# A fused two-layer hybrid attention model: latent queries and keys made by feature instead of by token, their scores split into 64-row and 32-row tiles

## What is computed

```python
q = (_rmsnorm(c_q, q_norm) @ w_uq).reshape(bsz, seq, MLA_HEADS, MLA_NOPE + MLA_ROPE)   # 192 -> 8 x (64 + 32)
kv = (_rmsnorm(c_kv, kv_norm) @ w_ukv).reshape(bsz, seq, MLA_HEADS, MLA_NOPE + MLA_V)  # 128 -> 8 x (64 + 64)
q = jnp.concatenate([q[..., :MLA_NOPE], _rope(q[..., MLA_NOPE:], positions)], -1)
k_r = jnp.broadcast_to(_rope(k_rope[:, :, None, :], positions), (bsz, seq, MLA_HEADS, MLA_ROPE))
k = jnp.concatenate([kv[..., :MLA_NOPE], k_r], -1)
o_mla = _dense_causal_attention(q, k, kv[..., MLA_NOPE:], (MLA_NOPE + MLA_ROPE) ** -0.5, None)
```

## Time and profile before

| | before |
|---|---|
| median of 3 runs, us | 854.97 (854.80 to 855.01) |
| the profiled execution, us | 854.98 |
| its span in the trace, us | 853.24 |
| TensorE matmul busy | 838.6 us, 98% |
| TensorE weight loads busy | 782.6 us, 92% |
| VectorE busy | 608.9 us, 71% |
| ScalarE busy | 467.3 us, 55% |
| mean granted TensorE clock | 0.997 |

### The profile page before, as it was taken

One profiled execution on the slowest core, in us unless ns is written; L12 is line 12 of the kernel. 1 busy time (PEld: TensorE's weight loads), 2 busy tenths in 40 slices (PEclk: granted clock), 3 DMA queues, 4 the chain that ended last, 5 costly groups with the idle time before them and its releaser, 6 DMA issues.

```text
span 853.2 us, 15785 instructions
## 1 busy us (share of the span) xinstructions
PE 838.6 (98%) x6364; PEld 782.6 (92%) x6364; DVE 608.9 (71%) x1099; ACT 467.3 (55%) x714; POOL 93.4 (11%) x112
## 2 busy tenths in 40 slices
PE   7999999999999999999999999999999999999996
PEld 6899999999899999988889999999998999999885
DVE  4775777887786877765667659688878777777554
ACT  5556767664355655553437377676634465555430
POOL 1002900004500000000000155000071000000000
PEclk9999999999999999999999999999999999999998
DMA  9757443344677777465845664334356787664631
GB/s 306 201 169 241 149 141 107 108 141 158 189 198 199 197 198 197 161 222 180 265 126 152 195 204 149 122 126 135 130 182 184 192 217 195 193 193 146 239 122 49
DMA packets 176407, 148.86 MB, mean 174 GB/s; under 512 B 18156, under 2 KB 149840, under 8 KB 176336
## 3 DMA queue, kind: packets, MB, share of 16 engines
q1 hardware_dynamic: 171712, 143.08, 55.0%
q10 hardware_dynamic: 4624, 4.78, 1.9%
HBM read 146.53 MB, written 1.05 MB: 173 GB/s over the span
## 4 chain that ended last, share of the span: by engine, by line
PE 95%; DVE 3%; ACT 0%; issue 0%; DVEq 0%; POOL 0%; ACTq 0%; POOLq 0%
PE ps L644 29%; PE ps L646 28%; PE ps L645 28%; PE ps L929 3%; PE ps L960 2%; PE ps L941 2%; DVE w_lo L1453 1%; PE ps L702 1%; PE ps L908 0%; PE ps L877 0%; PE ps L909 0%; PE ps L895 0%; PE ps L1026 0%; DVE x_tok L1677 0%; ACT w_hi L1123 0%
## 5 line engine op out<-in xcount | busy, mean ns | idle before, releaser
L1453 DVE TENSOR_TENSOR w_lo<-raw,w_hi 128x2048 fp32r<-128x2048 f32 (+3 forms) x142 | 304.7, 2148 | 111.2 <-ACT w_hi L1123 111.1
L644 PE MATMUL ps<-xt_hi,w_hi 128*128 128x256 f32 x1232 | 346.1, 281 | 0.7 <-ACT fq_t L1148 0.7
L645 PE MATMUL ps<-xt_lo,w_hi 128*128 128x256 f32 x1232 | 341.4, 277 | 0.0
L646 PE MATMUL ps<-xt_hi,w_lo 128*128 128x256 f32 x1232 | 341.3, 277 | 0.0
L1123 ACT ACTIVATE w_hi<-raw 128x2048 fp32r<-128x2048 f32 (+3 forms) x142 | 252.5, 1784 | 75.6 <-PE ps L646 67.2
L644 PEld LDWEIGHTS ps<-xt_hi,w_hi 128*128 128x128 f32 x1232 | 231.7, 188 | 4.2 <-issue 3.2
L645 PEld LDWEIGHTS ps<-xt_lo,w_hi 128*128 128x128 f32 x1232 | 231.7, 188 | 0.1
L646 PEld LDWEIGHTS ps<-xt_hi,w_lo 128*128 128x128 f32 x1232 | 231.6, 188 | 0.0
L644 PE MATMUL ps<-w_hi,ht_hi 128*128 128x512 f32 x176 | 68.6, 390 | 0.0
L645 PE MATMUL ps<-w_lo,ht_hi 128*128 128x512 f32 x176 | 68.5, 389 | 0.0
L646 PE MATMUL ps<-w_hi,ht_lo 128*128 128x512 f32 x176 | 68.5, 389 | 0.0
(11 more groups left out here) (234 smaller groups left out, 1280.8 us busy)
## 6 DMA issues: line engine op xcount, KB each, us to landing
raw<-ffn_w_up SPq DMA_DIRECT2D x88, 512.0 KB, 5.1
raw<-w_in SPq DMA_DIRECT2D x84, 512.0 KB, 4.6
raw<-ffn_w_down SPq DMA_DIRECT2D x32, 512.0 KB, 4.2
raw<-w_branch SPq DMA_DIRECT2D x24, 512.0 KB, 4.7
raw<-w_out SPq DMA_DIRECT2D x16, 512.0 KB, 4.3
raw<-ffn_w_down SPq DMA_DIRECT2D x24, 256.0 KB, 3.0
ln_g<-ln_g ACTq DMA_DIRECT2D x4, 512.0 KB, 3.6
ln_b<-ln_b ACTq DMA_DIRECT2D x4, 512.0 KB, 5.4
```

The lines of the kernel that those rows point to most:

```text
L644: pe.matmul(dst, a_hi, b_hi, start=first, stop=False)
L645: pe.matmul(dst, a_hi, b_lo, start=False, stop=False)
L646: return pe.matmul(dst, a_lo, b_hi, start=False, stop=last)
L1453: ins = dve.tensor_tensor(panel_lo(l, p)[0:n, cols], panel_raw(l, p)[0:n, cols], panel_hi(l, p)[0:n, cols].bitcast(F32), ALU.subtract)
```

## The change

The 64 plain columns of each latent query and key are made by feature, like those of the other branches: `qn_t`, `kn_t` with two heads in one array of 128 rows, four arrays. Only the 32 rotated query columns are made by token (`q_rope`). The rotated key columns are copied four times side by side (`kr4`). In slot 6, four transposes of 128 columns turn `q_rope` into `qr_t` (four heads in each of two arrays, ordered so that a pair's two heads lie 64 rows apart); in slot 7, two transposes turn `kr4` into `kr_t`. ScalarE copies both (`rope_out`). A latent score is then the sum of a matmul with contraction 64 and one with contraction 32 into the same PSUM bank. `head_operands`, `head_out`, `q_tok`, `k_tok` and `qks` are gone. The two weight matrices are loaded in an order by kind of column, in runs of 256 and 128 bytes for the queries and of 256 bytes for keys and values. The core of the diff:

```diff
@@ -544,12 +547,13 @@
             if p == UQ_AT:
-                return [(s[0:n, c:c + H * QK],
-                         w_uq[bass.ds(l, 1), r:r + n, :].rearrange("a p n -> p (a n)"))
-                        for n, r, c in ((P, 0, 0), (QR - P, P, H * QK))]
+                return [(by_head(s[0:n, c + to:c + to + H * w], w),
+                         w_uq[bass.ds(l, 1), r:r + n, :].rearrange("a p (h n) -> (a p) h n", n=QK)[:, :, at:at + w])
+                        for n, r, c in ((P, 0, 0), (QR - P, P, H * QK)) for to, at, w in ((0, 0, HD), (H * HD, HD, ROPE))]
@@ -814,15 +818,19 @@
+                parts = [(kk, whi[:, c:c + H * QK], wlo[:, c:c + H * QK]) for c, kk in ((0, 0), (H * QK, 2))]
+                rope = slice(H * HD, H * QK)
                 for t in range(NT):
                     tok = slice(P * t, P * t + P)
-                    for c in range(2):
-                        for half, kk in enumerate((0, 2)):
-                            cols = slice(H * QK * half + 384 * c, H * QK * half + 384 * c + 384)
-                            ins = product(ps[:, B_Q[t][c], 0:384], c_hi[:, kk, tok], c_lo[:, kk, tok],
-                                          whi[:, cols], wlo[:, cols], half == 0, half == 1)
-                    if t == 0:
-                        ins.then_inc(s_mla_q_product, 1)
+                    for kk, hi, lo in parts:
+                        ins = product(ps[:, B_ROPE, T * t:T * t + T], c_hi[:, kk, tok], c_lo[:, kk, tok],
+                                      hi[:, rope], lo[:, rope], kk == 0, kk == 2)
+                ins.then_inc(s_mla_q_product, 1)
+                for j in range(4):
+                    cols = slice(P * j, P * j + P)
+                    for kk, hi, lo in parts:
+                        ins = product(two_tiles(B_NOPE[j // 2])[:, j % 2, :], hi[:, cols], lo[:, cols],
+                                      c_hi[:, kk, :], c_lo[:, kk, :], kk == 0, kk == 2)
@@ -831,14 +839,16 @@
-                for c in range(2):
-                    for t in range(NT):
-                        tok = slice(P * t, P * t + P)
-                        cols = slice(512 * c, 512 * c + 512)
-                        ins = product(ps[:, B_KV[c][t], :], c_hi[:, 1, tok], c_lo[:, 1, tok],
-                                      whi[:, cols], wlo[:, cols], True, True)
-                        if c == 0 or t == 0:
-                            ins.then_inc(s_mla_kv_product, 1)
+                for t in range(NT):
+                    tok = slice(P * t, P * t + P)
+                    product(ps[:, B_VALUES[t], :], c_hi[:, 1, tok], c_lo[:, 1, tok], whi[:, 512:1024], wlo[:, 512:1024],
+                            True, True).then_inc(s_mla_kv_product, 1)
+                for j in range(4):
+                    cols = slice(P * j, P * j + P)
+                    ins = product(two_tiles(B_NOPE[j // 2])[:, j % 2, :], whi[:, cols], wlo[:, cols],
+                                  c_hi[:, 1, :], c_lo[:, 1, :], True, True)
@@ -896,18 +906,20 @@
-            def head_operands(l, h):
...
-                for t in range(NT):
-                    pe.transpose(ps[0:QK, B_QK, P * t:P * t + P], q_tok[:, t, QK * h:QK * h + QK], ident[:])
-                    ins = pe.transpose(ps[0:QK, B_QK, T + P * t:T + P * t + P], k_tok[:, t, QK * h:QK * h + QK], ident[:])
-                ins.then_inc(s_head_turned, 1)
+            def rope_operands(l, keys):
+
+                if not keys:
+                    pe.wait_ge(s_queries_rotated, at("queries_rotated", l, 1))
+                    pe.wait_ge(s_features_by_act, at("features_by_act", l, 10))
+                    for g in range(2):
+                        for t in range(NT):
+                            ins = pe.transpose(ps[:, B_QK, T * g + P * t:T * g + P * t + P], q_rope[:, t, P * g:P * g + P], ident[:])
                 else:
+                    pe.wait_ge(s_rotated, at("rotated", l, 1))
+                    pe.wait_ge(s_rope_ready, at("rope_ready", l, 1))
+                    for t in range(NT):
+                        ins = pe.transpose(ps[:, B_QK, P * t:P * t + P], kr4[:, t, :], ident[:])
+                ins.then_inc(s_rope_turned, 1)
@@ -916,18 +928,22 @@
                 for t in range(NT):
+                    toks, keys = slice(P * t, P * t + P), slice(0, P * (t + 1))
                     for a in range(2):
                         if b == MLA:
-                            q, k = qks[0:QK, a, 0, :], qks[0:QK, a, 1, :]
+                            q, k = spread_rows(qn_t, a)[:, j, :], spread_rows(kn_t, a)[:, j, :]
...
-                        ins = pe.matmul(ps[:, B_S[a], SPAN[t]], q[:, P * t:P * t + P], k[:, 0:P * (t + 1)],
-                                        start=True, stop=True)
+                        ins = pe.matmul(ps[:, B_S[a], SPAN[t]], q[:, toks], k[:, keys], start=True, stop=b != MLA)
+                    for a in range(2):
+                        if b == MLA:
+                            rows = slice(HD * a + ROPE * (j % 2), HD * a + ROPE * (j % 2) + ROPE)
+                            ins = pe.matmul(ps[:, B_S[a], SPAN[t]], qr_t[rows, j // 2, toks], kr_t[rows, keys], start=False, stop=True)
@@ -1338,19 +1352,22 @@
+                        act.wait_ge(s_mla_q_product, at("mla_q_product", l, 1))
                         for t in range(NT):
...
-                            act.activation(q_tok[:, t, :].rearrange("p (c n) -> p c n", c=2),
-                                               ps[:, B_Q[t][0]:B_Q[t][1] + 1, 0:384], ACT.Copy, scale=-QK ** -0.5).then_inc(s_mla_q_ready, 1)
+                            for g in range(2):
+                                cols = slice(P * g, P * g + P)
+                                ins = act.activation(q_rope[:, t, cols].rearrange("p (a j n) -> p j a n", j=2, a=2),
+                                                     two_tiles(B_ROPE)[:, t, cols].rearrange("p (j a n) -> p j a n", j=2, a=2),
+                                                     ACT.Copy, scale=-QK ** -0.5)
+                        ins.then_inc(s_mla_q_ready, 1)
+                        act.wait_ge(s_panel_used, at("panel_used", l, UQ_AT + 1))
+                        act.activation(qn_t[:].rearrange("p (b i) t -> p b (i t)", b=2), ps[:, B_NOPE[0]:B_NOPE[1] + 1, :], ACT.Copy,
+                                       scale=-QK ** -0.5).then_inc(s_mla_q_ready, 1)
```

More of the change, by code:

```diff
@@ L96 @@
 B_FEAT = (6, 7)
-B_Q = ((0, 1), (2, 3))
-B_KV = ((0, 1), (2, 3))
+B_NOPE, B_ROPE = (0, 1), 2
+B_VALUES = (2, 3)
 B_CUM = 4
@@ L336, in build_program @@
                 mg_lo = so("mg_lo", [P, KD, T], F32R)
-            q_tok = sa("q_tok", [P, NT, H * QK])
-            k_tok = sa("k_tok", [P, NT, H * QK])
+            qn_t = sa("qn_t", [P, 4, T])
+            kn_t = sa("kn_t", [P, 4, T])
+            qr_t = sa("qr_t", [P, 2, T])
+            kr_t = sa("kr_t", [P, T])
+            q_rope = sa("q_rope", [P, NT, H * ROPE])
             v_tok = sa("v_tok", [P, NT, H * HD])
@@ L546, in halves @@
             if p == UQ_AT:
[L547 to L549 removed]
+                return [(by_head(s[0:n, c + to:c + to + H * w], w),
+                         w_uq[bass.ds(l, 1), r:r + n, :].rearrange("a p (h n) -> (a p) h n", n=QK)[:, :, at:at + w])
+                        for n, r, c in ((P, 0, 0), (QR - P, P, H * QK)) for to, at, w in ((0, 0, HD), (H * HD, HD, ROPE))]
             if p == UKV_AT:
[L551 to L552 removed]
+                return [(by_head(s[:, 512 * i:512 * i + 512], HD),
+                         w_ukv[bass.ds(l, 1), :, :].rearrange("a p (h n) -> (a p) h n", n=2 * HD)[:, :, HD * i:HD * i + HD])
+                        for i in (1, 0)]
             if p < BR_AT:
@@ L918, in scores @@
                     pe.wait_ge(s_index_relu_ready, at("index_relu_ready", l, NT))
-                if b == MLA:
-                    pe.wait_ge(s_head_ready, at("head_ready", l, 2 * j + 2))
+                if b == MLA and j == 0:
+                    pe.wait_ge(s_rope_ready, at("rope_ready", l, 2))
                 for t in range(NT):
+                    toks, keys = slice(P * t, P * t + P), slice(0, P * (t + 1))
                     for a in range(2):
                         if b == MLA:
-                            q, k = qks[0:QK, a, 0, :], qks[0:QK, a, 1, :]
+                            q, k = spread_rows(qn_t, a)[:, j, :], spread_rows(kn_t, a)[:, j, :]
                         elif b == FOX:
@@ L1182, in gate, with rope_out @@
                                    scale=0.5, bias=bg2[:, s:s + 1]).then_inc(s_gate_ready, 1)
-            def head_out(l, h):
-                act.wait_ge(s_head_turned, at("head_turned", l, h + 1))
-                if h >= 2:
-                    act.wait_ge(s_scores_ready, at("scores_ready", l, 4 + h // 2))
-                act.activation(qks[0:QK, h % 2, :, :], ps[0:QK, B_QK, :].rearrange("p (a t) -> p a t", a=2),
-                               ACT.Copy).then_inc(s_head_ready, 1)
+            def rope_out(l, keys):
```

(23 more changed lines are left out.)

54 lines of the change are left out of this document (24 added, 30 removed).

## The result

| | before | changed |
|---|---|---|
| median, us (6 runs each, on one chip) | 854.54 (853.87 to 855.01) | 858.35 (857.30 to 858.66) |
| the profiled execution, us | 854.98 | 858.57 |
| its span in the trace, us | 853.24 | 856.7 |
| mean granted TensorE clock | 0.997 | 0.998 |

The ratio is 1.0044, 95% interval 1.0033 to 1.0055: the change costs 2.8 to 4.7 us. The forecast was +2.2 us, 857.2 us, slower; direction and range hold, and the size was about 1.5 us short.

The account below looks back on a forecast made before the run. It took TensorE's own instruction list as the bound. Transposes −5.7, scores +7.6, product step +0.2 and queries and keys +0.1 gave +2.2 us on 854.98, so 857.2 us, range 851.9 to 858.9.

Parts of the forecast that it names:

- The frame: TensorE's own list sets the time, other engines' work costs nothing without new waits; wrong if TensorE's waits grew a microsecond.
- Transposes, −5.7: Slots 6 and 7: 12 transposes in all instead of 64, at 0.11 us each, save 5.7 us.
- Scores, +7.6: Latent scores: five tile-height changes cost 0.95 us more a pair, over 8 pairs 7.6 us; array time unchanged.
- Rivals 1 and 2: Latent scores: changes between 64 and 32 rows are free (852.4 us, chance 0.25) or half price (854.8 us, chance 0.13).
- Queries and keys, +0.1: Query and key products: 36 query matmuls of 256 columns replace 24 of 384; 0.1 us more for both, both layers.
- The step of the products, +0.2: Gate tiles: slots 11 and 15 turn slower, slot 7 faster, 0.10 us a tile; 0.2 us more in two layers.
- Rival 3: Gate tiles after the new scores take the slower step, 8 more a layer: 1.6 us more, 858.8 us; chance 0.08.
- Rival 4: Slot 7: key transposes wait for ScalarE's copy of slot 6's query transposes; 861 us at worst, chance 0.02.

Follow-up runs that it names:

- e5: Changed kernel with four unread transposes put ahead of the values of slots 10 and 14; 859.24 us.
- e4: Changed kernel with the latent score rounds reordered to plain, rotated, rotated, plain; 855.54 us.
- e2: Changed kernel with the rotated part in 64-row tiles, rotated keys standing twice with zeros in the other head's 32 rows; 853.17 us.
- e6: Changed kernel with rotated rows copied into the free half of a 128-row operand, so a latent score is one full-height matmul; 849.43 us.
- e7: Changed kernel with query and key/value weights loaded in whole rows, as before the change, so latent operands use wrong columns; 858.02 us.
- e1: Changed kernel with the rotated part (32-row matmuls) of the latent scores left out; 847.55 us.
- e8: Changed kernel with one unread transpose put behind the scores of slots 9, 11, 13 and 15; 858.58 us.
- e9: e6 with the eight transposes of rotated queries and keys one slot earlier; 849.59 us.

## Why the prediction was right, and where it was short

*The frame.* The bound is TensorE's own list, before and after. ScalarE lost 7.5 us (forecast: some 6) and VectorE 1.1, and nobody was faster for it. The waits grew by 0.7 us in single pieces outside the slots, less than the microsecond that would have broken the frame. Two readings in this part of the prediction were incomplete. Past the start TensorE waited three times before the change, not twice: a wait of 0.4 us for `vec_t` at 33.66 us is missing from the earlier trace rows, and it is the same after the change. And TensorE's rate is not one throughout: products of 432 columns follow each other at 0.36 us up to 11.9 us before and up to 10.6 after, at 0.20 from there on, though the granted clock reads 1.00 in these stretches.

*Transposes, −5.7.* Right. L916 and L921 occur 8 and 4 times in the changed kernel, 0.11 apart, and e5 paid 0.45 for four put back.

*Scores, +7.6.* Right to the hundredth of a microsecond in a pair, and shown piece by piece: five changes cost 0.95. The value chosen for the unseen change between 64 and 32 rows, 0.20, was an argued choice with no row behind it. It was then measured: four changes instead of five took off 0.20 (e4), two instead of five took off 0.60 (e2), and none took off all 0.95 (e6). This is also the answer to the rule of the Trainium skill that the prediction weighed, in "TensorEngine Tiling (Array Packing)", Tiling Modes, Key Properties: 64-row and 32-row tiles are separate modes, and a change between them drains TensorE like any other. The trace agrees that such a change has a price, 0.20 us for each; whether the array empties in it no row shows. Rivals 1 and 2, which held 0.38 of the chance, are excluded: the scores of a pair take 2.11 us, not 1.5 or 1.8.

*Queries and keys, +0.1.* The query products take 4.30 and 4.31 us in the two layers, 0.12 a matmul, where 4.18 and 4.24 stood before: +0.2. The keys' products take 2.83 in each layer, where 2.79 stood: +0.1. Together 0.3, three times the forecast. e7 shows that it is not the loads.

*The step of the products, +0.2.* This is where the forecast fell short, by the size of a term and not by its sign. I let slots 11 and 15 become slow and slot 7 fast, and had the tiles after the new scores stay fast. Slots 7, 11 and 15 came as I said. But slots 8 and 9 became slow behind the transposes of slot 7 (in e1 as well, without any new scores), and slots 12, 13, 16 and 17 behind the new scores (gone in e1 and in e4, still there in e2). That is seven tiles net in each layer instead of one, 14 × 0.108 = 1.5 us in place of 0.2, and these 1.3 us are most of what the forecast lacked. Rival 3, with 0.08 of the chance, had eight more tiles in each layer. It was miscounted: between the new scores and the next interruption stand six, those of slots 10, 12, 13, 14, 16 and 17, worth 1.3 us and not 1.6. Six more than in the forecast's account did come, but 8 and 9 in place of 10 and 14, so the nearness of its total, 858.8, to the measured one is luck. Its mechanism as I put it, a step that depends on the kind of interruption, didn't stand up (e5, e8), and the 11 and 15 that I had right were right by luck: e5 puts the transposes back ahead of both, and 11 stays slow.

*Rival 4*, a new wait in slot 7, did not appear: the key transposes start 0.12 after the last product, at 116.39.

What is still open: which property of the instruction list sets the step. It is the same in both layers in all eleven kernels, so it isn't chance. One transpose more in each latent slot changes six tiles of a layer (e8), eight transposes moved by a slot change none (e9). It depends on more than the last interruption and the step before it: in the changed kernel the same latent scores and transposes turn a slow tile into a fast one at slot 10 and leave it slow at slot 12.

## What to carry to other kernels

Count the changes of tile height on TensorE, not only passes: each was worth 0.20 us here, as much as two transposes or a float32 pass over 256 columns, so a matmul split over two heights inside a loop gives back quickly what smaller tiles save. Padding an operand with zeros to the full height cost nothing in the scores (1.31 us a pair, as with 96 rows) and two more transposes a layer; order the work so that equal heights stand together, or fill the height. When a TensorE-bound kernel is forecast to better than 0.2%, add a term for the products' step, with a width of one tile's difference (0.1 us here) for every tile behind the first place that changes: tiles far from it changed as well.

## What the runs showed of the hardware that I had not expected

- The products of 256 columns run in the slots at one of two steps, 0.1133 and 0.1178 us (22 steps in 2.49 or 2.59), fixed between two interruptions and identical from layer to layer, and in e7 as in the changed kernel, which have the same list there. Some tiles take 2.51 or 2.52: their first four or five steps are 0.116 to 0.122 and the others 0.113 (e6, slots 7 and 10). Four tiles at the other step are 0.43 us a layer; e4's slots show 0.38 a layer beyond its four pairs' 0.20 each.
- A change between 64 and 32 rows costs just what entering from the whole array costs, 0.20 us, and it shows as 0.10 on the first round and 0.10 on the second. Adding to a bank already begun costs nothing beside the columns: 0.22 us for the two adding rounds of 128 columns in e2.
- Contraction 128 with 32 rows of zeros takes 1.31 us for a pair of heads, as contraction 96 did.
- ScalarE's copy of 64 rows × 1024 columns takes 1.02 us (e6), and one of 128 rows × 1024 columns 1.05 (`qn_t` in the changed kernel): half the rows don't make it shorter.
- Runs of 128 and 256 bytes in the loads of two panels a layer, 28460 packets under 512 bytes in place of 18156, made no difference that these runs can show (e7).
